# Decay and rate projections of both scan directions in joint groups of 128-column pieces, at new places in the turn

## What is computed

```
k = z[..., OFF_K:OFF_V];  v = ...;  kk = normalised (k * k_k) per head
for d, (ow, oa) in enumerate(((OFF_WF, OFF_AF), (OFF_WB, OFF_AB))):
    lw    = w0[d] + tanh(z[..., ow:ow+64]) @ w_up[d]            # "decay projection"
    decay = exp(-exp(-softplus(-lw) - 0.5))
    a     = sigmoid(a0[d] + z[..., oa:oa+64] @ a_up[d])         # "rate projection"
    k_d   = k * (1 + (a - 1) * k_a)
    ... (decay, k_d, kk * a) go into the scan of direction d
```

## Time and profile before

| | |
|---|---|
| median of 3 runs | 4067.24 us (4062.73 to 4070.47) |
| the profiled execution's own time | 4079.55 us |
| its span, first to last instruction | 4077.7 us |
| mean granted TensorE clock | 0.986 of full speed |
| busy: PE, PEld | 95%, 62% of the span |
| busy: DVE, ACT, POOL | 41%, 28%, 14% |
| TensorE instructions | 51352 matmuls, 51352 weight loads |
| pair phases | about 80 to 1045 us and 2319 to 3225 us |

### The profile page before, as it was taken

The page is one execution under the profiler, slowest core; times in us unless marked ns, Lnnn a source line. Parts: engine busy times, 40 slices in busy tenths (PEclk is TensorE's granted clock), DMA queues, the critical chain, the costliest instruction groups (busy, mean ns, idle before and its releaser), DMA issues.

```text
span 4077.7 us, 111806 instructions
## 1 busy us (share of the span) xinstructions
PE 3880.4 (95%) x51352; PEld 2546.8 (62%) x51352; DVE 1687.0 (41%) x2721; ACT 1146.1 (28%) x2003; POOL 551.5 (14%) x436
## 2 busy tenths in 40 slices
PE   7899999999999999999999988999998999999998
PEld 3566666666555555655555556666666556678887
DVE  2555566664862111322231254555555422122232
ACT  3444444442122000200000344444444221021001
POOL 0000000000032221122232000000000023213443
PEclk8999999999999999999999999999999999999999
DMA  5000000000333223211112300000010253242224
GB/s 205 25 9 24 25 25 25 25 22 28 108 131 104 93 88 95 79 61 62 52 62 73 123 25 9 23 23 23 23 34 21 68 194 114 83 144 92 85 89 129
DMA packets 76337, 277.40 MB, mean 68 GB/s; under 512 B 8672, under 2 KB 13024, under 8 KB 75488
## 3 DMA queue, kind: packets, MB, share of 16 engines
q1 hardware_dynamic: 67968, 235.96, 18.1%
q10 hardware_dynamic: 6624, 29.04, 1.9%
q0 software_dynamic: 1280, 5.24, 0.3%
HBM read 256.58 MB, written 13.63 MB: 66 GB/s over the span
## 4 chain that ended last, share of the span: by engine, by line
PE 90%; ACT 4%; issue 3%; DVE 2%; DMA 1%; POOL 0%; ACTq 0%; DVEq 0%; SPq 0%; POOLq 0%
PE psum L1156 17%; PE psum L1670 16%; PE psum L1040 12%; PE psum L741 11%; PE psum L1467 9%; PE psum L1602 6%; PE psum L1052 5%; PE psum L1562 3%; PE psum L1625 2%; PE psum L1188 2%; PE psum L732 2%; PE psum L1000 2%; DMA ring<-w_stream_in 1%; PE psum L1018 1%; PE psum L921 1%
## 5 line engine op out<-in xcount | busy, mean ns | idle before, releaser
L1156 PEld LDWEIGHTS psum<-arena 32*32 32x32 f32 (+3 forms) x40512 | 697.6, 117 | 375.4 <-issue 301.4
L1156 PE MATMUL psum<-arena 32*32 32x32 f32 (+4 forms) x40512 | 790.8, 208 | 105.4 <-issue 73.7
L1040 PE MATMUL psum<-arena,ring 128*128 128x512 f32 (+1 forms) x1408 | 573.1, 523 | 2.5 <-ACT arena L1858 1.6
L741 PE MATMUL psum<-arena,ring 128*128 128x512 f32 (+1 forms) x1264 | 463.1, 524 | 3.8 <-DVE arena L2552 3.8
L741 PEld LDWEIGHTS psum<-arena,ring 128*128 128x128 f32 x1264 | 238.8, 191 | 230.3 <-issue 200.7
L1670 PE MATMUL psum<-arena 128*128 128x384 f32 (+1 forms) x1344 | 368.6, 433 | 0.0
L1040 PEld LDWEIGHTS psum<-arena,ring 128*128 128x128 f32 x1408 | 239.2, 191 | 142.0 <-issue 115.5
L1670 PEld LDWEIGHTS psum<-arena 128*128 128x128 f32 x1344 | 255.4, 190 | 106.4
L2991 POOL DMA_DIRECT2D ya_spill<-arena x16 | 8.8, 550 | 1995.2 <-DVE arena L2552 1995.2
L1670 PE MATMUL psum<-arena,ring 128*128 128x384 f32 (+1 forms) x1008 | 278.5, 433 | 0.0
L1670 PEld LDWEIGHTS psum<-arena,ring 128*128 128x128 f32 x1008 | 191.6, 190 | 79.5
(11 more groups left out here) (175 smaller groups left out, 4428.6 us busy)
## 6 DMA issues: line engine op xcount, KB each, us to landing
ring<-w_stream_in SPq DMA_DIRECT2D x440, 512.0 KB, 3.8
x_spill<-arena ACTq DMA_DIRECT2D x2, 3072.0 KB, 8.7
arena<-x_spill ACTq DMA_DIRECT2D x16, 384.0 KB, 6.5
arena<-ya_spill ACTq DMA_DIRECT2D x6, 768.0 KB, 6.0
ring<-w_stream_in ACTq DMA_DIRECT2D x8, 512.0 KB, 6.4
arena<-x_in ACTq DMA_DIRECT2D x1, 3072.0 KB, 14.3
arena<-ups_in SPq DMA_DIRECT2D x16, 192.0 KB, 2.4
ya_spill<-arena POOLq DMA_DIRECT2D x8, 384.0 KB, 6.3
```

The source lines that it names most:

```text
L741: mm = eng.matmul(psum[0:lhs[k].shape[-1], tile, a - off:b - off], lhsT=lhs[k], rhs=rhs[k][:, a:b], start=(k == 0), stop=(k == len(lhs) - ...
L1040: mm = pe.matmul(bank(j, z=b - a), lhsT=w[k], rhs=hs[k][:, a:b], start=(k == 0), stop=(k == KT - 1))
L1156: return pe.matmul(out, lhsT=lhs, rhs=rhs, start=start, stop=stop, skip_group_check=True)
```

## The change

The eight projections of a turn become three groups, each issued as one step of stream `d` by a new function, up_group:

- FIRST: decay, half 0 (512 columns), both directions;
- BOTH: decay, half 1, and rate, half 1 (256 columns each), both directions, side by side in the bank;
- LAST: rate, half 0, both directions.

Inside a group the matmuls are pieces of 128 columns, direction 0 and direction 1 by turns, that is upper and lower rows by turns. Direction 0 writes bank 0 and direction 1 bank 1; in turn 0 the groups take banks 2 to 7 instead. A group is eight pieces. It waits until both banks are free, and each bank is released by the last gate that reads it. ACT and DVE steps are reordered: k's second half is copied before the decay gates, r's first half before gates 2 and 3, r_shift(0) comes before the scans on DVE. The norm tiles move up in the dense stream. WEAVE's strings for PE change in turns 1 to 7 of both layers, and DVE's for turn 1 of layer 1; all others stay, so there the reordered steps fall into the old places.

```diff
-UP_ORDER = ((0, 0), (1, 1), (1, 0), (0, 1))
+UP_ORDER = dict(lw=((0, 0), (1, 0), (0, 1), (1, 1)), la=((0, 1), (1, 1), (0, 0), (1, 0)))
+UP_GROUPS = dict(first=(("lw", 0, 0),), both=(("lw", 1, 0), ("la", 1, 256)), last=(("la", 0, 0),))
+UP_BANK = dict(first=2, both=4, last=6)
...
+        def up_bank(t, group, d):
+            return d + (0 if t else UP_BANK[group])
...
-                def up_tile(t, name, ev, src, n, reader, j):
...
-                        yield from single(name, ev, g, j, half, ups_block(g, n, side(d)), slot(src)[side(d)], reader.at(g, j), True)
...
+                def up_group(t, group):
...
+                    name, half, at = UP_GROUPS[group][-1]
+                    for d in DIRS:
+                        hold(up_bank(t, group, d), (sw if name == "lw" else sa).at(g, UP_ORDER[name].index((d, half))))
+                    for name, half, at in UP_GROUPS[group]:
+                        (a, b), n, src, ev = HALVES[half], "lw la".split().index(name), LW if name == "lw" else LA, lw if name == "lw" else la
+                        for c in range(a, b, P):
+                            for d in DIRS:
+                                mm = pe.matmul(bank(up_bank(t, group, d), a=at + c - a, z=at + c - a + P), lhsT=ups_block(g, n, side(d)),
+                                               rhs=slot(src, c, c + P)[side(d)], start=True, stop=True, skip_group_check=True)
+                                if c + P == b:
+                                    mm.then_inc(ev.sem, 1)
+                    yield
...
                     yield from k_tiles(t, 1, 2, 4)
-                    yield from decay_tile(t, 0)
                     yield from k_tiles(t, 1, 4, 6)
-                    yield from decay_tile(t, 1)
                     yield from k_tiles(t, 1, 6, 8)
-                    yield from decay_tile(t, 2)
+                    yield from up_group(t, "first")
                     yield from r_tiles(t, 0, 0, 2)
-                    yield from decay_tile(t, 3)
                     yield from r_tiles(t, 0, 2, 4)
-                    yield from rate_tile(t, 0)
                     yield from r_tiles(t, 0, 4, 6)
-                    yield from rate_tile(t, 1)
                     yield from r_tiles(t, 0, 6, 8)
+                    yield from up_group(t, "both")
                     yield from r_tiles(t, 1, 0, 2)
-                    yield from rate_tile(t, 2)
+                    yield from norm_tile(t, 0)
                     yield from r_tiles(t, 1, 2, 4)
-                    yield from rate_tile(t, 3)
-                    yield from norm_tile(t, 0)
+                    yield from norm_tile(t, 1)
                     yield from r_tiles(t, 1, 4, 6)
-                    yield from norm_tile(t, 1)
                     yield from r_tiles(t, 1, 6, 8)
+                    yield from up_group(t, "last")
...
                     yield from raw_k_half(0)
+                    yield from raw_k_half(1)
                     yield from decay_gate(0)
                     yield from decay_gate(1)
-                    yield from raw_k_half(1)
-                    yield from decay_gate(2)
-                    yield from decay_gate(3)
+                    yield from raw_r_half(0)
...
+                    yield from decay_gate(2)
+                    yield from decay_gate(3)
                     yield from rate_gate(0)
                     yield from rate_gate(1)
-                    yield from raw_r_half(0)
+                    yield from raw_r_half(1)
                     yield from rate_gate(2)
                     yield from rate_gate(3)
-                    yield from raw_r_half(1)
...
                     yield from k_shift(1)
+                    yield from r_shift(0)
                     if prep:
...
-                    yield from r_shift(0)
                     yield from norm_max(0)
```

More of the change, by code:

```diff
@@ L186 @@
 WEAVE.update((("PE", 1, t), (
-    "ddddxsdxxssxsddxdssxdxxdddddddssdddsxdxsdsxdddddssdddsddsdssdsdssdsddxddsdsxddddsddssssssddsdssssssd"
-    "sssssssdssssssssssssssssssssssssss")) for t in (1,))
+    "ddddxsdxxssxsddxdssxdxxddddddddssdxsddxsddsxsdddddssdssssdssdsddxddsdsxddddsddssssssddsdssssssdsssss"
+    "ssdssssssssssssssssssssssssss")) for t in (1,))
 WEAVE.update((("PE", 1, t), (
-    "xxsssdsxssxxdxxddddsxdsdxsddddsdddsdddsdddxsdsddsddsddsddsddsxdsddsxdsdsddxsddddsddsdsssddssdsssssds"
-    "ssdssssdddsssssssssssssssssssssssssss")) for t in range(2, KT))
+    "xxsssdsxssxxdxxddddsxdsdxsddddsddddddssdxsdddsdddddssdxssdsxdssdsdsddxsddddsddsdsssddssdsssssdsssdss"
+    "ssdddsssssssssssssssssssssssssss")) for t in range(2, KT))
 WEAVE.update((("PE", 1, t), (
@@ L645, in state_sum, with up_result @@
             return bank((6 if n < 8 else 4) + d, rows, n % 8 * C, n % 8 * C + C)
+        def up_bank(t, group, d):
+            return d + (0 if t else UP_BANK[group])
+        def up_result(t, name, j):
+            d, half = UP_ORDER[name][j]
+            group, at = [(k, at) for k, parts in UP_GROUPS.items() for n, h, at in parts if (n, h) == (name, half)][0]
+            a, b = HALVES[half]
+            return bank(up_bank(t, group, d), a=at, z=at + b - a)
         def wk(c, rows=slice(0, P), a=0, b=P):
@@ L1087, in bonus_tile @@
                         yield from single("bonus", bonus, g, j, j, heads, slot(BN + g % 2), bv.at(g, j), False)
-                def up_tile(t, name, ev, src, n, reader, j):
[L1090 to L1096, removed]
-                        yield from single(name, ev, g, j, half, ups_block(g, n, side(d)), slot(src)[side(d)], reader.at(g, j), True)
-                def decay_tile(t, j):
-                    yield from up_tile(t, "lw", lw, LW, 0, sw, j)
-                def rate_tile(t, j):
-                    yield from up_tile(t, "la", la, LA, 1, sa, j)
+                def up_group(t, group):
+                    if t >= KT:
+                        return
+                    g = KT * l + t
+                    pe.wait_ge(ups[g % 3], 16 * (g // 3 + 1))
+                    if t == 0 and group == "first":
+                        pe.wait_ge(*phases["lora"]["A"].end(l))
+                        pe.wait_ge(*phases["lora"]["V"].end(l))
+                    name, half, at = UP_GROUPS[group][-1]
[10 more added lines that the diff above has]
+                    yield
                 def norm_tile(t, j):
@@ L1865, in rate_gate @@
                                 act.wait_ge(*sv.at(g - 1, 3))
-                            d, half = UP_ORDER[j]
+                            d, half = UP_ORDER["la"][j]
                             act.wait_ge(*la.at(g, j))
                             tables(SIGMOID)
-                            act.activation(slot(SA + d, *HALVES[half]), landed("la", j, half), ACT.Sigmoid, bias=vec(f"a0{d}", t)).then_inc(sa.sem, 1)
+                            act.activation(slot(SA + d, *HALVES[half]), up_result(t, "la", j), ACT.Sigmoid, bias=vec(f"a0{d}", t)).then_inc(sa.sem, 1)
                             yield
```

18 lines of the change are left out of this document (9 added, 9 removed).

## The result

The changed kernel takes 4155.71 us (median of 4 runs, 4152.46 to 4159.22) where the kernel before, on the same chip, takes 4067.74 us: ratio 1.0218, 95% interval 1.0200 to 1.0236, so 81 to 96 us slower. On a second chip the ratio was 1.0199 (1.0180 to 1.0218), 73 to 89 us. The forecast was 61 us slower, with a range of -7 to +98 us. The execution profiled here took 4153.99 us (span 4152.2), 74.4 us more than the profiled one of before.

A forecast was written before the change was run, and what follows sets the result against it. TensorE's own time and its gaps were taken to bound the kernel. Work and waits +5, starved issue +46 and clock +10 made 61 us on 4067.2, so 4128 us; range 4060 to 4165 us.

The forecast's parts named there:

- TensorE's work: Turns 0 to 7 of each layer: merged projections and fewer runs of one shape take 86 us off TensorE.
- slow clock: After idle stretches TensorE runs at half speed more often: +10 us, bounds nothing and 36 us.
- waits for results: TensorE waits longer for DVE and ACT, mainly at norm tile 1: +91 us, or +5 with the work removed.
- issue: Small products put together in turns 2 to 7 outrun the instruction supply: +46 us, bounds 0 and 60.
- fewer changes of shape: Turns 2 to 7: 15 fewer runs of one shape on TensorE, 3.15 us less a turn.
- The wait at `r0.0`: Turns 2 to 7 of layer 0: TensorE waits 1.0 us until decay gate 0 gives bank 0 back.
- The one at LAST: Turns 2 to 7 of layer 0: TensorE waits 0.7 us at LAST for raw_r(1) on ACT.
- the walk: Stepping the three queues through a turn with the trace's durations to get waits and issue idle; trusted to some tenths.
- the waits feed the queue: Rival: instructions arrive while TensorE waits for L2446, so today's issue idle vanishes; -53 us, 4014 us; chance 0.12.
- Waits only: Rival: starved issue costs what it costs today, leaving +5 us, 4072 us; chance 0.16.
- Halves not side by side: Rival: the groups' pieces stream one after the other in all 16 turns; +41 us, 4169 us; chance 0.06.
- The clock falls in nearly every turn: Rival: the slow clock costs +36 us in place of +10, 4154 us; chance 0.12.

The follow-up runs named there:

- e2_norm_first: The changed kernel with norm_max(0) ahead of the two scans on DVE; ratio 1.0101 to the kernel before, 40 to 48 us faster than the changed kernel.
- e4: The changed kernel with four dense products that nobody reads ahead of the group BOTH in turns 1 to 7; ratio 1.0261 to the kernel before.
- e1: The changed kernel with all pieces of direction 0 issued before those of direction 1 in each group; ratio 1.0252 to the kernel before.
- e6: The changed kernel with one full-width product per direction and half in place of 128-column pieces; ratio 1.0214 to the kernel before.

## Why the prediction was right, and which terms were off

It was right in sign and range, and low: 61 us forecast, 73 to 96 measured. By its own steps, on the profiled executions:

| term | forecast | measured |
|---|---|---|
| TensorE's work | -86 | -79 to -87 |
| slow clock | +10 | +62 to +69 |
| waits for results | +91 | +53 |
| issue | +46 | +40 |
| together | +61 | +74.5 |

- **The clock is the failed step.** It lay outside its own bound of 36 us. Every clock record of these traces stands at 1.00 or 0.50 of full speed, so the mean granted clock gives the time at the lower level: (1 - 0.986) x 2 x 4077.7 = 114 us before, (1 - 0.965) x 2 x 4152.2 = 291 us after. Not all of it is work: summed over those stretches, TensorE is busy in them for 87.6 us before and 226.5 after, 138.9 more. What a busy microsecond at that level costs comes from e2_norm_first, which has the same matmuls as the changed kernel: 178.7 us there, 47.8 less, go with 21.2 us less busy, 0.44 each. It can't be over 0.5, since the level is half. So the clock costs 62 to 69 us, and with the 17.7 us that busy time fell the work removed is 79 to 87. This is an estimate. My error was to bound the clock by one slow stretch of 3 us a turn and to call it "partly hidden". Measured between the copies of yv, each of the twelve turns 2 to 7 has 10 to 27 us at the lower level, 188 us in all, where before eight of them had none, and all twelve together 20 us. Turn 3 above has it from `tm3.1` to LAST: at 408.46, 418.90 and 422.58, where 0.50, 0.66 and 0.50 were granted, each time behind idle time of 0.9 to 2.2 us.
- **Work.** The projections take 72.6 + 45.0 = 117.6 us of TensorE before and 69.1 us after, part of that at the slow clock: 48.5 us less, where 16 x 2.5 = 40 were forecast. The other 46 us, fewer changes of shape, cannot be read from a row; by the estimate above 30 to 39 us are left for them. The Trainium skill, TensorEngine Tiling (Array Packing), Key Properties, says that a change of tiling mode drains TensorE; no run here tests that by itself.
- **Waits.** Place and cause held: L2462 in every turn. The size did not: 3.86 and 4.73 us in the turns 0 against 4.3 and 5.2 forecast, but in turns 2 to 7 an average of 2.4 us in layer 0 (14.4 in six turns) and 3.9 in layer 1 (23.4) against 2.9 and 6.1. The forecast took the overlap with starved issue off the issue term; the trace takes it off here. The wait at `r0.0` did not show: decay gate 0 ended at 390.18 us, and TensorE, held up by 1.18 us of issue, came to `r0.0` at 390.37. The one at LAST did, 5.6 us in six turns.
- **Issue.** The step that the walk gave best: 1.5 us for `tm2.0` to `um2.0` (forecast 1.5), 8.5 us for `tm3.0` to `um3.1` (8.8), with 222 matmuls in stock at its start (190). The walk took a block of 128 every 3.8 us where its row gives 4.1; in the changed kernel TensorE resumed at 403.25 and 406.72, 3.5 us apart, with 128 matmuls between.
- **Turns 0 and 1** gained 1.9 us in layer 0 and 0.6 in layer 1, from the first matmul of the pair phase (80.92 and 2319.28 us before, 80.21 and 2367.73 after) to the first copy; 1.2 gained and 0.2 lost were forecast.

The rivals: *the waits feed the queue* has a true core, since in e2 over half of the wait that it removed came back as issue. But it is an exchange, and e4 shows that the stock does not last. The rule of the Trainium skill (Runtime: NRT & Kernel Launch, Instruction fetch mechanics) that block boundaries are mostly hidden does not hold for these stretches: 117.2 us of issue idle stand in the trace. *Waits only* falls by the 39.6 us of issue. *Halves not side by side* falls by e1 and e6. *The clock falls in nearly every turn* was given 0.12 and is what happened, in all twelve turns and at more than its price; had it been the forecast, with the walk's other terms as they were, it would have said 87 us.

The error has one more side: the sum came near partly because idle was 44 us too dear and the clock 52 to 59 us too cheap. That is luck. An idle stretch cost its own length and then the slow stretch behind it, and of the second I counted hardly anything.

## What to carry to other kernels

Where TensorE's small matmuls come faster than their instructions, the order of small and dense steps can undo all that a merger saves: here two orders of the same steps lie 88 to 96 us apart, where the merger takes some 80 us of work off TensorE and the two directions side by side are worth 15 to 20 of them. Before putting such steps together, count the matmuls in each run of them, and see whether any step in that order feeds an engine that TensorE will wait for a few steps later. Price an idle stretch together with the slow clock behind it.

## What the runs showed of the hardware that I had not expected

- Two fp32 products of 512 columns, one on each half of the rows, take 1.13 us together (e6_wide, 388.79, `64x512` x4), where one alone takes 1.12 us. No cutting into pieces is needed. Four pieces of one direction and then four of the other take 1.71 us.
- Work that nobody reads, 59.8 us of it, made the kernel no slower (1.0184 against 1.0218 and 1.0199). The Trainium skill, TensorE: Matmul & The Clock Gate, HAM oscillation, tells of a matmul kernel in which every short burst between DMA waits starts at the lower clock. Here the waits are for issue and for DVE; the rows of turn 3 agree in kind, 1.91, 2.75 and 2.08 us against 1.03, 1.89 and 1.16 at the upper level.
- Splitting 16 x 8 projections into pieces cost 10 us in the kernel before, and not as issue idle: 3.7 us stand in their own rows, the rest goes with more busy time at the lower clock level. What lowers the clock there is open.
